# Routing the first tile's heads in two portions in every pass of a hybrid encoder kernel

## The reference, cut to what matters

```python
q = (xt @ w_query).reshape(T, PEER_HEADS, 2, PEER_HALF)
s = jnp.einsum('thsk,snk->thsn', q, sub_keys)
sv, si = lax.top_k(s, PEER_TOPK)                       # the search: 16 best keys of each half
cand = (sv[:, :, 0, :, None] + sv[:, :, 1, None, :]).reshape(T, PEER_HEADS, PEER_TOPK * PEER_TOPK)
cv, ci = lax.top_k(cand, PEER_TOPK)                    # the routing: 16 best pairs
i1 = jnp.take_along_axis(si[:, :, 0], ci // PEER_TOPK, axis=-1)
i2 = jnp.take_along_axis(si[:, :, 1], ci % PEER_TOPK, axis=-1)
idx = i1 * PEER_N_KEYS + i2
g = jax.nn.softmax(cv, axis=-1)                        # the gates
hid = jax.nn.gelu(jnp.einsum('td,thkd->thk', xb, expert_u[ib]), approximate=False)
out = jnp.einsum('thk,thkd->td', gb * hid, expert_v[ib])
```

## Time and profile before

| | |
|---|---|
| median of 3 runs | 4046.07 us (4044.48 to 4049.7) |
| profiled execution, first to last instruction | 5878.7 us |
| mean granted TensorE clock in it | 0.555 of 2.4 GHz |
| TensorE busy | 5726.4 us (97%) |
| VectorE busy | 2887.4 us (49%) |
| ScalarE busy | 1648.5 us (28%) |
| GpSimd busy | 1285.3 us (22%) |
| moved by DMA | 1444 MB, mean 246 GB/s |

### The profile page before, as it was taken

The page is one execution under the profiler, slowest core; times in us unless marked ns, Lnnn a source line. Parts: engine busy times, 40 slices in busy tenths (PEclk is TensorE's granted clock), DMA queues, the critical chain, the costliest instruction groups (busy, mean ns, idle before and its releaser), DMA issues.

```text
span 5878.7 us, 40315 instructions
## 1 busy us (share of the span) xinstructions
PE 5726.4 (97%) x13374; PEld 2787.7 (47%) x13374; DVE 2887.4 (49%) x5745; ACT 1648.5 (28%) x4216; POOL 1285.3 (22%) x1094
## 2 busy tenths in 40 slices
PE   9999999999999998999999999899999999899999
PEld 5555555444444545444445545344445555222222
DVE  3321003665555455756555555756555554744443
ACT  3431101344422211244432211245422211222222
POOL 0000000222222221322222221322222221334343
PEclk6555555555555555555555555555555555555555
DMA  4222222767777775767777775777777775899997
GB/s 155 93 102 81 73 90 95 267 238 266 261 275 268 274 280 202 285 245 280 273 272 297 283 291 190 280 256 271 271 268 308 281 290 191 315 350 342 345 342 281
DMA packets 212948, 1444.45 MB, mean 246 GB/s; under 512 B 27256, under 2 KB 27256, under 8 KB 46340
## 3 DMA queue, kind: packets, MB, share of 16 engines
q0 software_dynamic: 164976, 1133.94, 52.0%
q1 hardware_dynamic: 47632, 307.80, 14.4%
q10 hardware_dynamic: 132, 0.12, 0.0%
HBM read 1439.31 MB, written 7.13 MB: 246 GB/s over the span
## 4 chain that ended last, share of the span: by engine, by line
PE 96%; DVE 2%; ACT 1%; issue 1%; DMA 0%; SPq 0%; ACTq 0%; DVEq 0%
PE banks L609 52%; PE sums L871 21%; PE banks L871 7%; PE banks L748 5%; PE banks L827 3%; PE banks L669 2%; PE banks L736 1%; PE banks L786 1%; PE banks L778 1%; PE banks L694 1%; PE banks L844 1%; DVE x L1479 1%; DVE rows L1470 0%; PE banks L637 0%; PE banks L700 0%
## 5 line engine op out<-in xcount | busy, mean ns | idle before, releaser
L609 PE MATMUL banks<-hT,ring 128*128 128x256 f32 x6656 | 2608.4, 583 | 4.7 <-DVE arena L1316 3.9
L609 PEld LDWEIGHTS banks<-hT,ring 128*128 128x128 f32 x6656 | 1507.5, 228 | 1151.7 <-issue 734.0
L576 POOL DMA_INDIRECT rows<-in_w_uv,idx x1024 | 1237.6, 1209 | 3600.3 <-PE sums L871 1981.3
L1470 DVE CUSTOM_DVE_ANT_0 rows<-rows,xn 128x1024 f32<-128x1024 f32 x1024 | 1241.6, 1220 | 530.8 <-DMA rows<-in_w_uv,idx 528.0
L871 PE MATMUL sums<-rows,diag 128*128 128x512 f32 x1612 | 1285.2, 970 | 70.0 <-ACT diag L1076 47.9
L1479 DVE SCALAR_TENSOR_TENSOR x<-rows,wgt,x 128x1024 f32<-128x1024 f32 x493 | 632.0, 1282 | 234.8 <-ACT wgt L1068 234.0
L871 PEld LDWEIGHTS sums<-rows,diag 128*128 128x128 f32 x1612 | 369.2, 232 | 791.7 <-issue 683.2
L1281 DVE SCALAR_TENSOR_TENSOR arena<-banks,pr,arena 128x254 f32<-128x254 f32 (+1 forms) x512 | 246.8, 482 | 354.6 <-ACT arena L965 340.9
L1063 ACT ACTIVATE gelu<-hid 128x2 f32<-128x2 f32 x512 | 102.9, 201 | 1100.7 <-DVE hid L1470 1099.3
L609 PE MATMUL banks<-yT,ring 128*128 128x256 f32 x1024 | 400.2, 582 | 0.0
L871 PE MATMUL banks<-rows,diag 128*128 128x512 f32 x512 | 393.7, 966 | 0.0
(11 more groups left out here) (205 smaller groups left out, 2955.8 us busy)
## 6 DMA issues: line engine op xcount, KB each, us to landing
ring<-in_w_ssd SPq DMA_DIRECT2D x96, 1024.0 KB, 5.4
ring<-in_w_att SPq DMA_DIRECT2D x64, 1024.0 KB, 6.1
ring<-in_w_mrg SPq DMA_DIRECT2D x52, 1024.0 KB, 8.4
arena<-a_rows POOLq DMA_DIRECT2D x32, 1024.0 KB, 7.6
ring<-in_w_qry SPq DMA_DIRECT2D x32, 1024.0 KB, 4.8
arena<-bias_tiles POOLq DMA_DIRECT2D x16, 1152.0 KB, 7.3
ring<-in_w_out SPq DMA_DIRECT2D x16, 1024.0 KB, 7.0
rows<-in_w_uv,idx POOLq DMA_INDIRECT x1024, 6.8
```

What stands on the lines that cost most here:

```text
L576: nc.gpsimd.indirect_dma_start(out=rows[n % NB][:, :], out_offset=None, in_=w_uv, in_offset=bass.IndirectOffsetOnAxis(ap=idx[:, t, s:s + 1 ...
L609: mm = pe.matmul(out, w[:, k * P:(k + 1) * P], rhs[:, k0 + k, :], start=start and k == 0, stop=stop and k == n - 1)
L1470: v.tensor_tensor_reduce(u, u, xn2[:, (n // SLOTS_T) % 3, :], 1.0, 0.0, ALU.mult, ALU.add, hid[:, k:k + 1]).then_inc(u_done, 1)
```

## The change

In every pass, not in the first alone, the first tile is routed in two portions of 4 heads, heads 0 to 3 and heads 4 to 7; the second tile stays one portion, so a pass has three. The first portion of passes 1 to 3 is routed in the query stage, two pieces after the search of each of heads 4 to 7 (`FIRST_PIECES`), its softmax and gates early in the route stage. The second portion of every pass is routed in the recurrence of the next pass, groups 0 and 1, with its softmax and gates in group 1; the second tile's ten pieces follow from group 1 to group 3, its gates stay in group 3. For the last pass both late portions go between ticks of the tail. The second portion gets its own key buffer (`second_keys`) and shares the second tile's scratch space. The table of ticks is dealt anew: ssd groups 0 and 1 get 20 for 22, att 70 for 65, mrg 44 for 42, out 13 for 11, query 12 for 13, route 14 for 20; the percentages stay. `FINALS`, the places of the final norms in the tail, move. In `route` the indices of key buffers become those of the portion (left out here).

```diff
-PARTS = [(0, 0, 0, 4), (0, 0, 4, 8)] + [(m, t, 0, 8) for m in range(PASSES) for t in range(2) if m or t]
+PARTS = [(m, *part) for m in range(PASSES) for part in ((0, 0, 4), (0, 4, 8), (1, 0, 8))]
...
-BESIDE = [("norm", 0, 1, 8, 60), ("ssd", 0, 2, 22, 80), ("ssd", 2, GROUPS, 70, 50), ("att", 0, 4, 65, 15), ("mrg", 0, 8, 42, 5),
-          ("out", 0, 1, 11, 0), ("norm2", 0, 1, 5, 100), ("query", 0, 2 * PH + 1, 13, 0), ("route", 0, REST, 20, 100)]
+BESIDE = [("norm", 0, 1, 8, 60), ("ssd", 0, 2, 20, 80), ("ssd", 2, GROUPS, 70, 50), ("att", 0, 4, 70, 15), ("mrg", 0, 8, 44, 5),
+          ("out", 0, 1, 13, 0), ("norm2", 0, 1, 5, 100), ("query", 0, 2 * PH + 1, 12, 0), ("route", 0, REST, 14, 100)]
...
-LATE_PIECES = [(), (0,), (1,), (2,), (), (3,), (4,), (), (5,), (6,), (7,), (), (8,), (9,), (), ()]
+FIRST_PIECES = {4: (0, 1), 5: (2, 3), 6: (4, 5), 7: (6, 7)}
+
+SECOND, THIRD = 1, 2
+LATE_PIECES = [((SECOND, 0), (SECOND, 1)), ((SECOND, 2),), ((SECOND, 3), (SECOND, 4)), ((SECOND, 5),),
+               ((SECOND, 6), (SECOND, 7)), (), ((THIRD, 0), (THIRD, 1)), ((THIRD, 2),),
+               ((THIRD, 3),), ((THIRD, 4),), ((THIRD, 5), (THIRD, 6)), (),
+               ((THIRD, 7),), ((THIRD, 8),), ((THIRD, 9),), ()]
 LATE_STEPS = 4
...
-LAST_ROUTE = 48
-FINALS = {64: (0, 0), 68: (0, 1), 140: (1, 0)}
+LAST_SECOND = {2 * n + 2: n for n in range(8)}
+LAST_SECOND_GATES = 24
+LAST_THIRD = {4 * n + 27: n for n in range(10)}
+LAST_ROUTE = 74
+FINALS = {80: (0, 0), 84: (0, 1), 140: (1, 0)}
...
         late_keys = sb("late_keys", [P, 4 * SLOTS_T])
+        second_keys = sb("second_keys", [P, 2 * SLOTS_T])
...
-                    if m and g == LATE_STEPS - 1:
+                    if m and g in (1, LATE_STEPS - 1):
                         yield place("ssd", g, 0.64)
-                        softmax(part_of(m - 1, SLOTS_T))
+                        softmax(3 * (m - 1) + (SECOND if g == 1 else THIRD))
...
-                yield place("route", REST - 1)
-                softmax(part_of(m, SLOTS_T - 1))
+                yield place("route", 2)
+                if m:
+                    softmax(part_of(m, 0))
...
                         if m and g < LATE_STEPS:
-                            for n in LATE_PIECES[4 * g + j]:
-                                route(part_of(m - 1, SLOTS_T), n)
+                            for of, n in LATE_PIECES[4 * g + j]:
+                                route(3 * (m - 1) + of, n)
...
                     if m == 0 and h == 3:
                         for n in range(PIECES_OF[4]):
                             route(0, n)
+                    if m:
+                        for n in FIRST_PIECES.get(h, ()):
+                            route(part_of(m, 0), n)
...
-                now = part_of(m, SLOTS_T - 1)
-                pieces = PIECES_OF[PARTS[now][3] - PARTS[now][2]]
-                for n in range(pieces):
-                    yield place("route", n * REST / pieces)
-                    route(now, n)
-                yield place("route", REST)
-                gates(now)
+                yield place("route", 3)
+                if m:
+                    gates(part_of(m, 0))
```

More of the change, by code:

```diff
@@ L397, in routing_room @@
             return cand, half, bits, b16, cvh, ci, over, over.bitcast(U16).rearrange("p (s k) -> p s k", s=2)
-        room = [routing_room(arena[:, late_room:while_heads]), routing_room(yT[:, 8:16, :].rearrange("p c t -> p (c t)"))]
+        late_place = routing_room(yT[:, 8:16, :].rearrange("p c t -> p (c t)"))
+        room = [routing_room(arena[:, late_room:while_heads]), late_place, late_place]
         used[0] = while_heads
-        v16x16 = [cut(4 * SLOTS_T), late_keys[:, :]]
-        work = [cut(4 * SLOTS_T), late_keys[:, :]]
-        v16 = [w[:, 0:2 * SLOTS_T].rearrange("p (h i k) -> p h i k", h=PH, i=2) for w in v16x16]
-        x16 = [w[:, 2 * SLOTS_T:].bitcast(U32).rearrange("p (h i k) -> p h i k", h=PH, i=2) for w in v16x16]
+        found = [cut(2 * SLOTS_T), second_keys[:, :], late_keys[:, :]]
+        work = [cut(2 * SLOTS_T), second_keys[:, :], late_keys[:, :]]
+        v16 = [w[:, 0:w.shape[1] // 2].rearrange("p (h i k) -> p h i k", i=2, k=TOPK) for w in found]
+        x16 = [w[:, w.shape[1] // 2:].bitcast(U32).rearrange("p (h i k) -> p h i k", i=2, k=TOPK) for w in found]
         pij = [w.bitcast(U32).rearrange("p (n k) -> p n k", n=4) for w in work]
         pf = [w.rearrange("p (n k) -> p n k", n=4) for w in work]
-        idh = [w[:, 0:2 * SLOTS_T].rearrange("p (n k) -> p n k", n=2) for w in work]
-        row = [w[:, 2 * SLOTS_T:3 * SLOTS_T] for w in work]
+        idh = [w[:, 0:w.shape[1] // 2].rearrange("p (n k) -> p n k", n=2) for w in work]
+        row = [w[:, w.shape[1] // 2:w.shape[1] // 4 * 3] for w in work]
         used[0] = spare
@@ L1090, in _ @@
                 tick(PASSES - 1, k)
-                if k == LAST_ROUTE - 2:
+                if k == LAST_SECOND_GATES - 3:
+                    softmax(len(PARTS) - 2)
+                if k == LAST_ROUTE - 3:
                     softmax(len(PARTS) - 1)
@@ L1135, in search @@
                 v.wait_ge(q_sv.sem, q_sv.at(m, h + 1))
-                best16(steps[0], [keys[:, t, 2 * h + i, :] for i in range(2)], [v16[t][:, h, i, :] for i in range(2)],
-                       [x16[t][:, h, i, :] for i in range(2)])
+                of = next(n for n in range(3) if PARTS[n][1] == t and PARTS[n][2] <= h < PARTS[n][3])
+                g = h - PARTS[of][2]
+                best16(steps[0], [keys[:, t, 2 * h + i, :] for i in range(2)], [v16[of][:, g, i, :] for i in range(2)],
+                       [x16[of][:, g, i, :] for i in range(2)])
                 steps[0] += 7
@@ L1145, in route @@
                 hs, ks = slice(lo, hi), slice(lo * TOPK, hi * TOPK)
-                cand, half, bits, b16, cvh, ci, over, iint = room[t]
+                of = n % 3
+                own, mine = slice(0, H), slice(0, H * TOPK)
+                cand, half, bits, b16, cvh, ci, over, iint = room[of]
                 def link(ins):
@@ L1350, in mixer @@
                             v.tensor_copy(aT[0:64], pb(4)[0:64, 256:512]).then_inc(dt_T.sem, 1)
-                    if m and g == LATE_STEPS - 1:
+                    if m and g in (1, LATE_STEPS - 1):
                         yield place("ssd", g, 0.66)
-                        gates(part_of(m - 1, SLOTS_T))
+                        gates(3 * (m - 1) + (SECOND if g == 1 else THIRD))
                     yield place("ssd", g, 0.95)
@@ L1502, in _ @@
                 tick(PASSES - 1, k)
-                if k % 4 == 2 and k // 4 < PIECES_OF[PH]:
-                    route(len(PARTS) - 1, k // 4)
+                if k in LAST_SECOND:
+                    route(len(PARTS) - 2, LAST_SECOND[k])
+                if k == LAST_SECOND_GATES:
+                    gates(len(PARTS) - 2)
+                if k in LAST_THIRD:
+                    route(len(PARTS) - 1, LAST_THIRD[k])
                 if k == LAST_ROUTE:
```

32 lines of the change are left out of this document (16 added, 16 removed).

## The result

The changed kernel takes 4105.9 us (median of 4 runs, 4101.73 to 4108.37) against 4046.2 for the kernel before beside it: ratio 1.014, 95% interval 1.0125 to 1.0154. It is slower by 1.4%, where the prediction had 4017 us and a range up to 4066.

The account below looks back on a forecast made before the run. Timed runs near the upper clock level, three limits close together, only the pass's end clearly VectorE's. The terms -70 + 8 + 33 = -29 us gave 4017 us from 4046, range 3976 to 4066.

Parts of the forecast that it names:

- part 3: Slots dealt elsewhere, into att, mrg and out: between nothing and 67 us in three passes, half taken, +33 us.
- part 1: End of passes: routing and ticks leave, 18.6 us a pass in passes 1 to 3, 14 in pass 0; -70 us.
- part 2: Recurrence: VectorE gets 10.6 us more a pass; between -15 and +32 us in three passes, middle taken, +8.
- VectorE sets these stretches: Condition of the 70 us gain at the ends of passes: VectorE is the limit there.
- I count it as not hidden: Query stage: the first portion's 13.67 us beside the search cost full time, as VectorE has no room to speak of.
- half of the groups have room: Recurrence: reason for taking the middle, +8 us; VectorE last in groups 0 and 3, 5 us of room in group 1.
- recurrence growing by over 10 us a pass: Sign in the recurrence: growth by more than 10 us a pass would show the prediction wrong.
- Part 4: Tail: three portions' pieces between ticks are hidden, 0 us; 0 to 5 us without that cover.
- TensorE bounds the timed runs: Rival: TensorE sets the timed runs too, at a clock between the two levels; 4009 us, chance 0.12.
- DMA sets the middle: Rival: in the middle of passes each slot costs its 2.48 us wherever it stands; 4028 us, chance 0.25.
- Slower: Rival: VectorE is last in the recurrence and in att, +32 and +67 against -70; 4075 us, chance 0.17.
- The change doesn't do what it says: Rival: in-order ScalarE delays evictions, so query grows by what route loses; 4046 us, chance 0.08.

Follow-up runs that it names:

- half the bytes: Kernel before and changed kernel, each with gathers of 4 KB rows in place of 8 KB from the ninth slot on: 3741.9 and 3725.3 us.
- the portions alone: The changed kernel's new portions with the old table of ticks, against the kernel before: 4092.8 us beside 4050.8 (ratio 1.0107).

## Why the prediction was wrong

By the windows the change came to +53.7 us where the sum had -29. Of these 83 us part 3 accounts for 48, part 1 for 32 and part 2 for 3: the steps that failed are the halved price of the slots in the middle and the gain at the ends, taken whole.

**Part 1 (-70, measured -38): the step that failed is "VectorE sets these stretches", taken for the whole of the gain.** In pass 0 the end fell by 10.8 us (14 predicted; 15.4 with half the bytes). In passes 1 to 3 the sum was 18.6 a pass; query and route together gave 7.6 and 8.8. The work did leave as summed: in the second pass VectorE is busy 18.5 us less in the two stages (131.8 to 113.3). But its wait for rows there rose by 8.2 us (1.5 to 9.7), and that is most of what is missing. I had read at the earlier trace rows that VectorE is late there and not asked by how much it leads what comes next. The answer is 1.5 to 3 us a pass: 20 ticks need 20 x 2.47 = 49 us of gathers, and the pieces lay beneath them. With half the bytes the same stretches gave 19.2 less 7.0, and VectorE still waited 4.4 us for rows, so the bytes are only part of it, and what else holds the rows back stays open. The piece on the first portion, "I count it as not hidden", was right, and worse than counted: without ticks beside the pieces few buffers come free, so the gathers slow down too (174 GB/s for 30 us).

**Part 2 (+8, measured +11): near, by luck, for the reason given does not hold.** VectorE's 14.3 us more in the recurrence came out as 14.1 (292.9 to 307.0), and as 10.6 with two slots fewer, as summed. The 14.1 cost 10 us a pass; with two slots fewer it was 3 to 4, +11 in all. But "half of the groups have room" does not hold: moving the pieces into the groups with idle time saved nothing. The line that would have been wrong, recurrence growing by over 10 us a pass, was just reached by the portions alone (9.8 to 10.2).

**Part 3 (+33): the term that was mis-sized.** It measured +80.7, above even its upper end of 67. I had 22.3 us of DMA for nine slots a pass and halved it because ten microseconds at 423 GB/s "needn't hold for a stage". They hold: att to norm2 move 419 GB/s over 426 us. And ten slots passed there rather than nine in the second and third pass (135 dot products for 125), though eight in the first. With half the bytes the same slots cost 18.8, so some 62 us go with the bytes and the rest does not. The earlier trace rows already had DMA as the longest of three in att, mrg and out; that comparison should have been believed at full price. The sentence that the prediction is wrong "if att, mrg, out grow by the full 22 us" is what happened.

**Part 4 (0): right.** The tail lost no time by the pieces: 647.9 us from its first dot product before, 645.2 after. The rest of the 17.6 us by which pass 3's route and tail are shorter is in the route stage, with six slots fewer there by the new table.

**The rivals.** "TensorE bounds the timed runs" falls: it is busy 3427.7 of 4048.5 us before and 29 us less after, and the time rose. "DMA sets the middle" had the mechanism of part 3, and came to 4028 because it let the ends keep their 18.6, gave the recurrence's two slots back at full price and had 22.3 us where the middle took 27. "Slower" was nearest in time (4075), but its mechanism in att, VectorE last, is not what the runs show: with half the bytes the same VectorE work costs 0 to 11 us a pass there, for 26 to 27. In the recurrence VectorE's work does cost time, as that rival had it. "The change doesn't do what it says" had one part right: query grew by 4 to 7 us, and in the second pass TensorE waited 3.9 us at one eviction of a query product that it did not wait for before.

**What was right in detail.** The timed runs are near the clock's upper level (0.944). 512 sums on VectorE, as foretold, and GpSimd's wait for indices at the pass's end, 12.8 us before, is gone; what that wait had cost was not tried. The group of the sums, and the wait of TensorE in the query stage named above:

```profile
L1496 DVE SCALAR_TENSOR_TENSOR x<-rows,wgt,x 128x1024 f32<-128x1024 f32 x512 | 655.6, 1280 | 18.1 <-ACT wgt L1080 17.5
```

```profile
PE banks L855 <- ACT yT L1057: 3.9, 1, 3.9
```

What stays open: which of VectorE's fixed waits in the recurrence makes its price 0.7 us per us; the runs show only that it is the same whether the pieces stand more in groups 0 and 3 or in groups 1 and 2. Nor does a run show why two slots fewer there take off 6 to 7 us a pass, more than their transfers.

## What to carry to other kernels

Before you move work off an engine that is late, ask how far behind it the next limit lies; here 8.8 us taken off VectorE gave 1.5 to 3, as it then waited for the gathers beneath. Where several stages share a stream of transfers, read in each stage how long the consumer waits for them: a slot moved into or out of a stage with such waits was worth 1.8 to 2.9 us here, about its transfer of 2.47, and four moved to where the engine stands idle with loaded buffers cost 1.7 in all. And idle time at fixed waits was little room for work placed elsewhere in an engine's program: of 14 us more work, 10 were paid.

## What the runs showed of the hardware

The DMA held its best rate for whole stages: mrg moved 425 and 426 GB/s over 133 and 148 us in the two kernels, and att to norm2 415 to 421 GB/s over 426 to 454 us, where ahead of the prediction I trusted 423 GB/s for ten microseconds only. The Trainium skill (DMA: Bandwidth & Descriptors, Specifications) gives some 358 GB/s as a core's share of HBM bandwidth; here, with one core at work, the measurement goes past it by almost a fifth, and the measurement decides. The windows of mrg, before and after:

```profile
2146.20:2279.20 133.00, 128.30 (x583) 110.83 (x581) 98.37 (x139) 49.72 (x102) 39.52 (x38) 0.99 1.01 425
2175.70:2324.00 148.30, 133.38 (x585) 113.25 (x584) 111.84 (x157) 51.40 (x105) 46.08 (x43) 0.94 1.01 426
```
